# Plain down products in the feed-forward blocks of a two-layer hybrid decoder, with two places per kind of gate/up weight block

## The reference

```python
D_MODEL, D_FF = 1024, 2816
def swiglu(h, w_gu, w_d):
    gu = h @ w_gu                                            # (T, 1024) @ (1024, 5632)
    return (jax.nn.silu(gu[..., :D_FF]) * gu[..., D_FF:]) @ w_d  # (T, 2816) @ (2816, 1024)
# each layer: x = x + swiglu(rms_norm(x, norm_ffn), w_gate_up, w_down)
```

## Time and profile before

| | us |
|---|---|
| median of 3 runs | 1297.5 |
| the profiled execution, its own time | 1297.56 |
| its span, first to last instruction | 1295.8 |
| PE busy | 1218.5 (94%) |
| DVE busy | 1068.0 (82%) |
| ACT busy | 684.7 (53%) |
| POOL busy | 283.3 (22%) |

### The profile page before, as it was taken

One profiled execution on the slowest core, in us unless ns is written; L12 is line 12 of the kernel. 1 busy time (PEld: TensorE's weight loads), 2 busy tenths in 40 slices (PEclk: granted clock), 3 DMA queues, 4 the chain that ended last, 5 costly groups with the idle time before them and its releaser, 6 DMA issues.

```text
span 1295.8 us, 26874 instructions
## 1 busy us (share of the span) xinstructions
PE 1218.5 (94%) x10559; PEld 1006.6 (78%) x10559; DVE 1068.0 (82%) x1795; ACT 684.7 (53%) x1179; POOL 283.3 (22%) x517
## 2 busy tenths in 40 slices
PE   9999998899999899999999999999789999998997
PEld 7767587778787778877888888887668778786886
DVE  6456668899999999877887787876779999998995
ACT  6233555565555544446555465554656555564443
POOL 1004300000001030047555555453000000110000
PEclk9999999899999999999999999999989999998999
DMA  8658565676767433330213322132657676763421
GB/s 268 219 170 290 169 163 144 156 199 161 205 169 163 111 121 103 135 114 34 82 50 99 91 74 82 50 99 93 173 144 189 168 195 177 183 151 88 131 90 66
DMA packets 69206, 180.39 MB, mean 139 GB/s; under 512 B 6841, under 2 KB 28857, under 8 KB 64858
## 3 DMA queue, kind: packets, MB, share of 16 engines
q1 hardware_dynamic: 56986, 152.73, 36.5%
q0 software_dynamic: 12096, 25.96, 12.6%
HBM read 167.56 MB, written 11.11 MB: 138 GB/s over the span
## 4 chain that ended last, share of the span: by engine, by line
PE 51%; DVE 22%; issue 10%; ACT 10%; DMA 6%; POOL 1%; SPq 1%; DVEq 0%; ACTq 0%; POOLq 0%
PE P L2565 20%; PE P L2614 10%; DVE wl L1772 7%; PE P L2192 7%; ACT wh L1056 4%; DMA arena<-w_gu 2%; DMA stage<-w_gu 2%; DVE arena L1817 2%; ACT arena L1089 2%; PE P L2803 2%; DVE arena L1836 1%; DVE wl L1970 1%; DVE stage L1754 1%; PE P L2789 1%; ACT arena L1088 1%
## 5 line engine op out<-in xcount | busy, mean ns | idle before, releaser
L2565 PE MATMUL P<-arena,wh 128*128 128x260 f16 x2288 | 395.4, 278 | 50.2 <-DVE arena L1791 28.9
L2565 PE MATMUL P<-arena,wl 128*128 128x260 f16 x1144 | 317.2, 277 | 0.0
L2565 PEld LDWEIGHTS P<-arena,wh 128*128 128x128 f16 x2288 | 222.0, 99 | 98.5 <-issue 49.2
L2565 PE MATMUL P<-zh,wh 128*128 128x260 f16 x704 | 193.6, 275 | 0.0
L2565 PE MATMUL P<-zh,wl 128*128 128x260 f16 x704 | 192.4, 273 | 0.0
L2565 PE MATMUL P<-zl,wh 128*128 128x260 f16 x704 | 192.3, 273 | 0.0
L1772 DVE SCALAR_TENSOR_TENSOR wl<-stage,wh 128x1024 f16<-128x1024 f32 (+2 forms) x142 | 155.0, 1093 | 12.7 <-ACT wh L1056 11.9
L1056 ACT ACTIVATE wh<-stage 128x1024 f16<-128x1024 f32 (+2 forms) x142 | 134.4, 948 | 52.1 <-PE P L2565 50.1
L1056 ACT ACTIVATE wh<-arena 128x1024 f16<-128x1024 f32 (+2 forms) x112 | 103.2, 922 | 104.7 <-PE P L2565 88.0
L1772 DVE SCALAR_TENSOR_TENSOR wl<-arena,wh 128x1024 f16<-128x1024 f32 (+2 forms) x112 | 117.9, 1053 | 16.3 <-ACT wh L1056 16.3
L2565 PEld LDWEIGHTS P<-arena,wl 128*128 128x128 f16 x1144 | 112.3, 98 | 18.2
(11 more groups left out here) (423 smaller groups left out, 2584.2 us busy)
## 6 DMA issues: line engine op xcount, KB each, us to landing
arena<-w_gu SPq DMA_DIRECT2D x56, 512.0 KB, 6.1
stage<-w_in SPq DMA_DIRECT2D x23, 1024.0 KB, 5.7
stage<-w_gu SPq DMA_DIRECT2D x44, 512.0 KB, 5.2
arena<-w_gu POOLq DMA_DIRECT2D x22, 512.0 KB, 5.6
stage<-w_gu POOLq DMA_DIRECT2D x22, 512.0 KB, 7.8
arena<-w_dn SPq DMA_DIRECT2D x12, 768.0 KB, 4.3
arena<-cache_k SPq DMA_DIRECT2D x32, 256.0 KB, 3.6
stage<-w_out SPq DMA_DIRECT2D x8, 1024.0 KB, 5.4
```

The costliest lines, as they stand in the source:

```text
L2565: mm = nc.tensor.matmul(bank, w[:, o:o + 128], x[:, k, :], start=(i in (0, 1, 3) and k == a and w is ringh and x is xh), stop=(k == z - 1 ...
```

## The change

- `PHASES` gets `dn0` and `dn1`: eight units each of one 128-wide output tile with 22 k blocks (2816 words per partition). Down becomes a plain product by `unit`, `product` and `leave_tile`; the last tile of layer 1 is done one token half after the other, with the final norm's work between.
- The seven-product loop keeps only the 11 gate/up steps. `gated` is one multiply; `high_part` and `gated_low` are one instruction each over both tiles, into `fh` and `fl`.
- `SLOTS` gives every kind of weight block two places (even and odd n), four of them in arena room that the seven down operands held. `ld11`, `ld21`, `ld22`, `ld_t1`, `ld_t3` are one semaphore for each kind. B22 of step 1 no longer uses `sq`.
- The first down unit is split in three pieces: two after products 68 and 69 (`down_piece`), the rest after the last gate/up product.
- In layer 1 the low part of the last `out1` unit is made after tile 3 instead of after tile 4 in DVE's list.
- Layer 1's and the masks' loads, POOL's `block_masks` and its set-up for layer 1 move to match.

```diff
-PHASES = (("in0", 8, 2, KD * 256), ("out0", 4, 2, KD * 256), ("in1", 16, 2, KD * 256), ("out1", 4, 2, KD * 256))
+PHASES = (("in0", 8, 2, KD * 256), ("out0", 4, 2, KD * 256), ("dn0", 8, 1, UNIT),
+          ("in1", 16, 2, KD * 256), ("out1", 4, 2, KD * 256), ("dn1", 8, 1, UNIT))
...
+        X4 = [arena[:, XS_AT + 1024 * i:XS_AT + 1024 * i + 1024] for i in range(4)]
+        SLOTS = {"B11": (S5[3], S5[0]), "B21": (S5[4], A3[1]), "B12": (X4[0], S5[1]), "T2": (X4[1], S5[2]),
+                 "T3": (A3[2], X4[2]), "B22": (A3[0], X4[3])}
...
             def ffn_loads(layer):
+                for kind in ("T3", "T1", "B22"):
+                    ffn_load(kind, 0, layer)
                 sp.wait_ge(hi_ready, FIRST_UNIT[out] + 4)
                 sp.wait_ge(lo_ready, FIRST_UNIT[out] + 4)
-                ffn_load("T1", 1, layer)
-                ffn_load("B11", 1, layer)
-                sp.wait_ge(c_lo, base + 2)
-                ffn_load("T3", 1, layer)
-                sp.wait_ge(ssq_ready, KD * (1, 3)[layer])
-                ffn_load("B22", 1, layer)
+                for kind, n in (("B11", 0), ("B21", 0), ("T1", 1)):
+                    ffn_load(kind, n, layer)
+                sp.wait_ge(mm_done, FIRST_TILE[out] + 5)
+                for kind in ("T3", "B22", "B11", "B21"):
+                    ffn_load(kind, 1, layer)
+                for n in range(2, NG):
+                    for kind, i in (("B11", 0), ("T3", 1), ("B21", 3), ("T1", 4), ("B22", 6)):
+                        sp.wait_ge(c_lo, base + conversion(7 * (n - 2) + i))
+                        ffn_load(kind, n, layer)
+                sp.wait_ge(c_lo, base + conversion(7 * (NG - 2) + 5))
+                down_load(0, layer)
+                sp.wait_ge(c_lo, base + conversion(7 * (NG - 1) + 3))
+                down_load(1, layer)
...
+            def high_part(p, layer):
+                act.wait_ge(prod_done, NG * layer + p + 1)
+                nc.scalar.activation(fh[:, 2 * p:2 * p + 2, :], gts[p % 2].rearrange("p (a t) -> p a t", a=2), ACT.Copy
+                                     ).then_inc(f_hi, 1)
...
                 for n in range(NG):
                     for i in range(7):
+                        k = 7 * n + i
+                        if i >= 3:
                             finals(n, i)
+                        for m in NEXT[k]:
                             convert(m, layer)
+                        if k in PIECES:
+                            down_piece(PIECES[k], k, layer)
+                        if n >= 1 and i == 0:
+                            gated(n - 1)
+                        if n >= 1 and i == 3:
+                            gated_low(n - 1)
...
+            def down(layer, until):
+                name = ("dn0", "dn1")[layer]
...
+                product(0, 0, 0, fh, fl, KF, 128, ready=ready).then_inc(mm_done, 1)
+                pe.wait_ge(f_fin, FINALS * (layer + 1))
+                unit(name, 0, 1, fh, fl)
+                phase(name, fh, fl, first=1, until=until)
...
+            last_tile(0, range(KF)).then_inc(f_mm, 1)
+            last_tile(1, range(0, 8))
+            pe.wait_ge(ssq_ready, 3 * KD + 7)
+            pe.wait_ge(rstd_ready, 4)
+            last_stat(0)
+            last_square(0)
+            last_tile(1, range(8, 18))
+            last_stat(1)
+            last_tile(1, range(18, KF)).then_inc(f_mm, 1)
+            last_square(1)
```

More of the change, by code:

```diff
@@ L345, in block_of @@
+        def ring(t, m):
+            return t[:, 1024 * RING[m]:1024 * RING[m] + 1024]
         def block_of(kind, n, layer):
             i, j = int(kind[1]) - 1, int(kind[2]) - 1
[L348 to L356, removed]
+            return w_gu[layer][2 * n + j][:, 1024 * i:1024 * i + 1024]
@@ L578, in ffn_load @@
             def ffn_load(kind, n, layer):
[L580 to L586, removed]
-                arrived = {"B11": ld1[n % 2], "T1": ld1[n % 2], "B22": ld2[n % 2], "B21": ld3, "T3": ld2[n % 2]}[kind]
@@ L674, in _ @@
             ffn_loads(1)
+            for u in range(2, 8):
+                down_load(u, 1)
             for c in range(2):
[L677 removed]
+                cs = slice(c * CH, (c + 1) * CH)
                 for j in range(4):
@@ L789, in _ @@
             ffn(0)
-            pool.wait_ge(f_mm, PRODUCTS)
-            pool.wait_ge(c_lo, NB7)
+            for l in range(LEVELS):
+                block_masks(l)
+            pool.wait_ge(mm_done, FIRST_TILE["in1"])
+            pool.wait_ge(c_lo, CONVERSIONS)
             nc.gpsimd.memset(rows[0:40, :], 0.0)
@@ L1850, in ffn_units, with gated, gated_low @@
-                for n in range(NU):
+                def gated(p):
+                    g = gts[p % 2]
+                    dve.wait_ge(silu_done, NG * layer + p + 1)
+                    dve.wait_ge(f_fin, fin + 10 * p + 10)
+                    nc.vector.tensor_tensor(g, g, uts[p % 2], MUL).then_inc(prod_done, 1)
+                def gated_low(p):
+                    dve.wait_ge(f_hi, NG * layer + p + 1)
+                    nc.vector.tensor_tensor(fl[:, 2 * p:2 * p + 2, :], gts[p % 2].rearrange("p (a t) -> p a t", a=2),
+                                            fh[:, 2 * p:2 * p + 2, :], SUB).then_inc(f_lo, 1)
@@ new lines, in ffn_units @@
+                        if n >= 1 and i == 3:
+                            gated_low(n - 1)
+                gated(NG - 1)
+                dve.wait_ge(hi_ready, FIRST_UNIT[name] + 1)
+                nc.vector.scalar_tensor_tensor(out=wl[:, 0, 2048:UNIT], in0=stage[:, 0, 2048:UNIT], scalar=WS,
+                                               in1=wh[:, 0, 2048:UNIT], op0=MUL, op1=SUB).then_inc(lo_ready, 1)
+                gated_low(NG - 1)
+                split_lo(FIRST_UNIT[name] + 1, 1, UNIT)
@@ new lines, in down @@
+            def down(layer):
+                name, b = ("dn0", "dn1")[layer], 2 * layer + 2
+                for i in range(4):
+                    for j in range(2):
+                        k = 2 * i + j
+                        if layer == 0 or k < KD - 1:
+                            leave_tile(name, k, k, j)
+                            if layer == 0:
+                                norm_lo(b, k)
+                            square_in(b, k)
+                        next_split(name, i, j)
@@ L1872, in out_phase @@
                     leave_tile(name, at, FFN_ROWS[layer][at], at % 2)
+                    if layer == 1 and at == 3:
+                        split_lo(FIRST_UNIT["out1"] + 3, 1, WORDS[FIRST_UNIT["out1"] + 3])
                     if at >= 1:
@@ L1878, in out_phase @@
                         next_split("out0", 0, at // 2)
-                    if layer == 1 and at == 4:
-                        split_lo(FIRST_UNIT["out1"] + 3, 1, WORDS[FIRST_UNIT["out1"] + 3])
                     if at == 5:
```

471 lines of the change are left out of this document (166 added, 305 removed).

## The result

| | before | after |
|---|---|---|
| median, us (4 runs each) | 1297.64 | 1260.94 |
| lowest to highest, us | 1296.2 to 1299.53 | 1260.1 to 1261.72 |
| ratio to before | | 0.9716 [0.9699, 0.9733] |
| span of the profiled execution, us | 1295.8 | 1258.6 |
| granted TensorE clock | 0.986 | 0.995 |

The account below looks back on a forecast made before the run. DVE's list was taken to pace 20 gate/up steps at 20.32 us. Terms 27.6 + 11.5 - 9.4 + 4.4 + 1.6 + 2.1 = 37.8 us off 1297.56 gave 1260 us, range 1252 to 1278 (8 in 10).

Parts of the forecast that it names:

- Steps 1 to 10: Gate/up steps after the first, both layers: five instructions leave DVE's list, PE paces at 18.65 us; gain 27.6 us.
- my walk: One gate/up step followed through DVE's list with PE never late: DVE needs 17.8 us, 1.45 us spare.
- Step 0: First gate/up step of each layer: shared semaphore's wait goes, 22.9 and 24.5 us; gain 11.5 us.
- The released wait and what is late next: In step 0, the 5.23 us hole at product 6 goes; the 3.3 us hole at product 2, from ACT's order, stays.
- Rival (b): Start of gate/up becomes load-bound, B11 costing ACT 4.5 us a layer and T1 another 3: 1275 us, chance 0.09.
- Down: Down of both layers: plain loop of 1056 matmuls instead of 924, 118.0 us without holes; cost 9.4 us.
- `in1`: Joint from down of layer 0 into `in1`: PE's 2.88 us wait and slow clock shrink; gain 4.4 us.
- `out1`: In `out1` PE waits 5.68 us for the last unit's split; moving it about 3 us ahead gains 1.6 us.
- Tail: At the end, one token half finishes 7 us before, so four of eight final pieces leave; gain 2.1 us.
- The loads: Gate/up loads: seven 512 KB DMAs a step as before, DMA share from 0.71 to 0.77; costed at nothing.
- My sign of a safe chain: In gate/up, T1's adding DMA landing more than 5 us ahead of T2 in the profile after.
- Rival (c): T1's load chain in gate/up outgrows its eight conversions (21.3 us): slower than before, 1305 us, chance 0.05.

Follow-up runs that it names:

- experiment 1: Changed kernel with DVE's removed work put back (all five instructions in layer 0, one in layer 1), results unused: 1268.11 us.
- experiment 2: Changed kernel with unused DVE work added in each gate/up step, 1.15 us in layer 0 and 1.76 us in layer 1: 1261.16 us.
- experiment 3: Kernel before with one edit, a semaphore of its own for T3's first term: 1282.11 us, ratio 0.9898.
- experiment 4: Changed kernel with ACT's two step 0 copies of product 0 moved before the last operand sums, DVE's block 3 low part before sum T4: 1254.32 us.
- experiment 8: Changed kernel run twice more, nothing edited: 1261.51 and 1258.39 us.
- experiment 6: Changed kernel with the last `out1` split back after tile 4 and PE waiting for all of `z` before `in1`: 1266.09 us.
- experiment 5: Changed kernel with the load of T1's first term issued three products later in layer 0, four in layer 1: 1269.99 us.
- the first repeat: First of the two unedited runs of the changed kernel in experiment 8: 1261.51 us.
- the second repeat: Second of the two unedited runs of the changed kernel in experiment 8: 1258.39 us.
- experiment 7: Kernel of experiment 4 with ACT's high part of the last `out1` unit moved ahead of the norm weights of tile 2: 1253.53 us.

## Why the prediction was right

**Steps 1 to 10** (predicted -27.6, measured -29.1). The rest of the list runs as in my walk, and the walk's 18.65 us is 18.67. Experiments 1 and 2 show the cause from both sides. The term was undersized by 1.5 us: I took 1.0 us of loss in each step 10, for the ring's three slots and DVE's two pieces, and there is none (+2.0), while 18.67 in place of 18.65 takes 0.5 back. DVE's list, put at 17.8 us, is 17.49.

**Step 0** (predicted -11.5, measured -9.6). The released wait and what is late next were named rightly (experiments 3 and 4). My 22.9 us in layer 0 assumed the full clock behind the 3.3 us hole, as the kernel before had it; it fell in the first profile and not in experiment 8's second run, where the two stages are 22.95 and 24.43 us against my 22.9 and 24.5. The hit in layer 1 is partly luck: my terms there add up to 24.65 and not 24.5, and I took 3.3 us for a hole that had been 2.61 and became 3.63. Rival (b) did not come: the load of B11 that I worried about landed at 195.40 in layer 0, 1.45 us before ACT wanted it, and ACT waited for no `w_gu` in either step 0.

**Down** (predicted +9.4). 1056 matmuls in 118.03 us in layer 0 are 0.1118 us each, the spacing of the earlier trace rows. The estimate of 98 ns between the two figures of the Trainium skill (TensorE: Matmul & The Clock Gate, Back-to-back issue gap) would have given 103.5 us; the trace has 118.0, so the measurement decides against it. Layer 1 cost 5.8 instead of 4.85 us: its stage was 113.3 and not 113.6 us before, and is 119.1 now, 118.0 for the matmuls and 1.1 for the statistics between them, of which I had counted 0.45. No tile change has a hole.

**The joints and the tail** (predicted -4.4, -1.6, -2.1). `in1`: 2.9 + 1.5, as stated. `out1`: -2.4. The wait shrank by the 3.1 us that the split moved; 0.4 us more of low clock behind it and 0.4 us more of a wait ahead of it took 0.8 back. Another 1.0 us came back in step 0, where the hole ahead of product 2 is 3.63 us long and was 2.61: with the split's old place it is 23.82 us (experiment 6), with the new one 24.77. That sits in step 0's row and looks like a smaller gain there. Net of that the split's new place gave 1.4 us from before to after, and 2.5 by experiment 6, against 1.6 predicted. Tail: -2.3.

**The loads** were costed at nothing, which held, but by less than I said. I expected the DMA share at 0.77 and it fell to 0.66 and 0.65: by length times GB/s the window of layer 0 moved 35.2 MB before and 31.6 MB now. The last steps had fetched seven blocks each for down as for gate and up; now two units of 1.44 MB take their place, which I had not counted. The adding DMAs' median grew all the same, from 6.0 to 8.3 us. On average 1.5 of SP's loads were under way beside one of them, and 0.8 in the kernel before; that this is the cause was not tested. My sign of a safe chain, T1 landing more than 5 us ahead of T2, failed in layer 0 (2.2 us at the least), without cost. Two terms were too kind: the time from T1's issue to T2 is 19.8 us in a steady step and not 21.3, since DVE makes the low parts of blocks 4 and 5 back to back, so the eighth conversion adds 1.14 us to the step's 18.67 and not 2.66, and the chain took 14.6 to 17.6 us in layer 0 where the medians of before gave 12.5. Rival (c) was nearer than its 0.05; experiment 5 shows what it costs.

**The sum.** -37.8 predicted, -37.2 measured in the spans. The terms' errors (+1.9 in step 0, +1.0 in down of layer 1, -1.5 in the steps, -0.8 in `out1`) nearly cancel, and the clock alone moves a run by up to 3.1 us (experiment 8), so a hit within 1 us is luck in part.

## What to carry to other kernels

Where two engines pace each other through a ring, compare the period of the slower one's list with the other's work: removing instructions pays until the lists are equal and nothing after, and the margin left (here 1.2 us a step) is what later edits may spend. A semaphore that counts two transfers of different age makes the younger one's fate everybody's; giving it its own was 12.6 us here, without any other edit. A wait that is shortened upstream may come back downstream when a third engine's list sets both, so follow that list to the next wait before counting the gain.

## What was unexpected in the hardware

The same hole in the same code is followed by the low clock in some executions and not in others. Behind the 3.41 to 3.43 us hole of layer 0's step 0, TensorE fell from 2.4 to 1.2 GHz in the changed kernel, in experiments 1, 3 and 6 and in the first repeat (24.55 to 24.63 us), and kept its full clock in experiments 2 and 5 and in the second repeat (22.95 to 22.97). In PE's timelines of the first profile and of the second repeat, equal instructions (a pair, then a single) advance by 0.65 and by 0.33 us, the low and the full clock:

```profile
214.72 0.64 PE L2453 MATMUL P<-arena,wh 128*128 128x260 f16 x2
215.15 0.42 PE L2453 MATMUL P<-arena,wl 128*128 128x260 f16 x1
215.37 0.64 PE L2453 MATMUL P<-arena,wh 128*128 128x260 f16 x2
```

```profile
214.69 0.39 PE L2453 MATMUL P<-arena,wh 128*128 128x260 f16 x2
214.91 0.27 PE L2453 MATMUL P<-arena,wl 128*128 128x260 f16 x1
215.02 0.38 PE L2453 MATMUL P<-arena,wh 128*128 128x260 f16 x2
```

The fall costs 1.6 to 1.7 us here. The kernel before kept its full clock behind this hole too (3.42 us long). Other holes do the same: behind the 2.7 us hole in `out1` the clock fell in the changed kernel, in experiments 2, 4 and 5 and in both repeats, and not in experiment 1, and behind the 3.0 us at `in1` it fell in the kernel before and not in experiment 3. The Trainium skill (TensorE: Matmul & The Clock Gate, What's actually happening) says of the start of a kernel that the same kernel shows different numbers of slow matmuls from run to run; these traces show the like in the middle of one. Three holes that add up to 2.1 us (step 0 of layer 0) did not bring the clock down in the profiles of experiments 4 and 7, and single ones of 2.6 to 2.8 us did in experiments 3, 6 and 7, while 2.5 us at `in1` in experiment 6 did not.
